# Down pages of experts 8 to 30 requested by ScalarE on its own queue, and another order of the last two experts

## What is computed

```python
def hierarchical_moe(x, wg, bg, we, be, w_gate, w_up, w_down):
    g_prob = softmax(xt @ wg + bg)                 # 4 groups of 8 experts
    g_top_p, g_idx = lax.top_k(g_prob, 1)
    e_top_l, e_idx = lax.top_k(e_logits, 2)        # two experts of that group
    gates = softmax(e_top_l) * g_top_p
    ...
    hb = silu(xb @ w_gate[e]) * (xb @ w_up[e])     # 1024 -> 512
    out = hb @ w_down[e]                           # 512 -> 1024
    ...
    return sum over each token's two experts of gate * out
```

## Time and profile before

| | us |
|---|---|
| three runs, median (lowest to highest) | 1268.96 (1267.98 to 1270.03) |
| the profiled execution | 1268.41 |
| its span, first to last instruction | 1266.7 |
| TensorE busy | 1040.9 (82%) |
| VectorE busy | 478.3 (38%) |
| ScalarE busy | 234.8 (19%) |
| chain that ended last: TensorE | 51% of the span |
| chain that ended last: DMA | 45% of the span |
| HBM traffic over the span | 364 GB/s |

### The profile page before, as it was taken

How to read it: one execution, slowest core, us unless ns; L and a number is a source line. 1 busy time by engine, 2 the same in 40 slices (tenths; PEclk the granted TensorE clock), 3 DMA queues, 4 the chain that set the end, 5 groups by cost and what they waited for, 6 DMA issues and landing times.

```text
span 1266.7 us, 22370 instructions
## 1 busy us (share of the span) xinstructions
PE 1040.9 (82%) x9525; PEld 704.6 (56%) x9525; DVE 478.3 (38%) x1230; ACT 234.8 (19%) x526; POOL 4.9 (0%) x27
## 2 busy tenths in 40 slices
PE   9999998866767575889999999999967675758676
PEld 7888755533433342448888888876533333425243
DVE  2342543532223222237665556464343222222223
ACT  2221121111111111103433333121111111111111
POOL 1000000000000000000000000000000000000000
PEclk9999998978788877899999999999988878878789
DMA  9888799999999999996676664899999999999997
GB/s 342 237 338 332 255 419 429 426 428 428 429 429 428 429 429 427 417 394 187 190 231 225 229 223 151 334 361 427 428 427 427 430 428 429 427 429 429 429 419 297
DMA packets 98305, 461.49 MB, mean 364 GB/s; under 512 B 17468, under 2 KB 60728, under 8 KB 73400
## 3 DMA queue, kind: packets, MB, share of 16 engines
q1 hardware_dynamic: 97872, 460.34, 90.5%
q10 hardware_dynamic: 360, 0.15, 0.0%
HBM read 459.38 MB, written 1.08 MB: 364 GB/s over the span
## 4 chain that ended last, share of the span: by engine, by line
PE 51%; DMA 45%; SPq 1%; DVE 1%; issue 1%; ACT 1%; POOL 0%; POOLq 0%; DVEq 0%; ACTq 0%
DMA front<-in_expert_w_up 39%; PE pa L1534 10%; PE pa L1829 8%; PE pb L1534 8%; DMA arena<-in_expert_w_down 5%; PE wa L1829 5%; PE acc L1565 4%; PE wb L1859 3%; PE acc L1684 2%; PE pb L1609 1%; SPq L362 1%; PE pb L1903 1%; PE wa L2124 1%; PE pb L1785 1%; PE acc L1869 1%
## 5 line engine op out<-in xcount | busy, mean ns | idle before, releaser
L1829 PE MATMUL pa<-front,arena 128*32 128x256 f32 x1792 | 126.6, 445 | 80.8 <-DMA front<-in_expert_w_up 80.8
L1289 DVE TENSOR_SCALAR lower<-lower 128x128 f32<-128x128 f32 x64 | 14.4, 225 | 417.6 <-ACT lower L606 417.6
L1829 PE MATMUL wa<-front,arena 128*32 128x256 f32 x1232 | 96.7, 479 | 88.5 <-DMA front<-in_expert_w_up 85.0
L1829 PEld LDWEIGHTS pa<-front,arena 128*32 128x32 f32 x1792 | 63.0, 128 | 146.9 <-DMA front<-in_expert_w_up 93.6
L1829 PEld LDWEIGHTS wa<-front,arena 128*32 128x32 f32 x1232 | 46.1, 136 | 142.1 <-DMA front<-in_expert_w_up 95.0
L606 ACT ACTIVATE arena<-wb 32x256 f32<-32x256 f32 (+2 forms) x236 | 88.9, 377 | 105.0 <-PE wb L1859 96.6
L1859 PE MATMUL wb<-w_dn,conv_raw 128*32 128x256 f32 x1472 | 87.9, 379 | 2.3 <-DMA w_dn<-in_expert_w_down 2.0
L1534 PE MATMUL pa<-hnT,w_x 128*128 128x256 f32 x384 | 85.1, 380 | 0.0
L1829 PE MATMUL wa<-w_x,arena 128*32 128x256 f32 x896 | 64.4, 451 | 19.1 <-DMA w_x<-in_expert_w_up 19.1
L1534 PEld LDWEIGHTS pa<-hnT,w_x 128*128 128x128 f32 x384 | 72.5, 190 | 10.0 <-issue 0.3
L1534 PE MATMUL pb<-hnT,w_x 128*128 128x256 f32 x336 | 74.5, 380 | 0.0
(11 more groups left out here) (345 smaller groups left out, 1252.0 us busy)
## 6 DMA issues: line engine op xcount, KB each, us to landing
w_dn<-in_expert_w_down SPq DMA_DIRECT2D x46, 2048.0 KB, 26.4
front<-in_expert_w_gate SPq DMA_DIRECT2D x42, 2048.0 KB, 19.1
front<-in_expert_w_up SPq DMA_DIRECT2D x42, 2048.0 KB, 23.6
w_x<-in_expert_w_gate SPq DMA_DIRECT2D x15, 2048.0 KB, 32.2
w_x<-in_expert_w_up SPq DMA_DIRECT2D x15, 2048.0 KB, 36.6
arena<-in_expert_w_down SPq DMA_DIRECT2D x14, 2048.0 KB, 25.8
w_x<-in_odd_in_proj SPq DMA_DIRECT2D x16, 1024.0 KB, 5.5
front<-in_expert_w_up SPq DMA_DIRECT2D x10, 1024.0 KB, 8.8
```

The source lines that it names most:

```text
L1289: link(v.tensor_scalar(eg, eg, 1.0, None, ALU.add))
L1829: ins = mm(gu[32 * j:32 * j + 32, :, :], xb[:, k, c0:c0 + CAP], w[k][:, :, P * j:P * j + P], start=(k == 0), stop=(k == KC - 1))
```

## The change

ScalarE gets a function `down_page(l, before)`. It asks, on ScalarE's own queue, for the down page that goes into the buffer of expert `before`, right after the copies of that expert's output. It covers positions 8 (`OWN`) to 30. SyncE keeps the down pages of positions 5 to 7 and of 31, and all gate and up pages; it no longer waits for down projections in between.

At the end of a layer SyncE asks for gate/up 30, then for gate/up 31 in two halves along the contraction (four of eight blocks each, gate and up of a half together), then for down 31. TensorE runs pass 29, down 28, down 29, sum 28, pass 30, sum 29, down 30, pass 31 in two halves with a wait each, sum 30, down 31, sum 31. The six warming matmuls are gone. ScalarE copies the output of position 30 after the Exp of 30, not after that of 31. The final norm's weights are asked for behind down 31 without the wait for its last half.

```diff
+OWN = 2 * QUAD
...
-                    for part in (2, 0, 1):
+                    for part in (2, 0, 1) if e < OWN else (0, 1):
                         expert_part(l, e, part, NE * l + previous(DSLOT if part == 2 else SLOT, e), which)
...
-                for parts in ((0, 1), (2,)):
-                    for e, which in last:
-                        for part in parts:
-                            expert_part(l, e, part, NE * l + previous(DSLOT if part == 2 else SLOT, e), which)
+                for part in range(2):
+                    expert_part(l, NE - 2, part, NE * l + previous(SLOT, NE - 2), last[0][1])
+                sp_.wait_ge(S["gu_done"], NE * l + previous(SLOT, NE - 1) + 1)
+                for half in range(2):
+                    k = slice(KC // 2 * half, KC // 2 * half + KC // 2)
+                    for part in range(2):
+                        w = (expert_w_gate, expert_w_up)[part][l, ds(last[1][1], 1), :, :]
+                        sp_.dma_start(w_gu[SLOT[NE - 1]][:, part, k, :],
+                                      w.rearrange("a (p k) f -> p (a k) f", k=KC)[:, k, :]
+                                      ).then_inc(S[("gu_res", "gu_in1")[half]], 16)
+                expert_part(l, NE - 1, 2, NE * l + previous(DSLOT, NE - 1), last[1][1])
...
-            sp_.wait_ge(S["dn_in3b"], 2 * uses(DSLOT, 3, NE) * 16)
...
+            def down_page(l, before):
+                for e in range(OWN, NE - 1):
+                    if previous(DSLOT, e) == before:
+                        which = act.value_load(order[0:1, NE * l + e:NE * l + e + 1], min_val=0, max_val=NE - 1)
+                        w = expert_w_down[l, ds(which, 1), :, :].rearrange("a (p j) n -> p (a j) n", p=P)
+                        d = DSLOT[e]
+                        dst = w_dn4 if d == 4 else w_dn[d]
+                        act.dma_start(dst[:, :, :], w).then_inc(
+                            (S["dn_in0"], S["dn_in1"], S["dn_in2"], S["dn_in2"], S["dn_in4"])[d], 16)
...
                         outputs_of(l, e - 1)
+                        if e - 1 != WIDE:
+                            down_page(l, e - 1)
...
-                    if e == NE - 1:
-                        output_alone(l, e - 1)
+                    if e == NE - 2:
+                        output_alone(l, e)
...
                         af(o_y, Y_ps, ACT.Copy).then_inc(S["w_act"], 1)
+                        down_page(l, WIDE)
...
+                    if e == NE - 1:
+                        pe.wait_ge(S["gu_res"], 48 * l + 48)
+                        gate_up(xs, CAP * j, gu_cols(s), GU[e % 2], ks=range(KC // 2))
...
+                    elif e == NE - 1:
+                        gate_up(xs, CAP * j, gu_cols(s), GU[e % 2], ks=range(KC // 2, KC)).then_inc(S["gu_done"], 1)
...
-                    if e and e != NE - 2:
+                    if e and e < NE - 2:
                         down_of(l, e - 1)
...
                     if e == NE - 2:
-                        warm(6)
+                        down_of(l, e)
```

More of the change, by code:

```diff
@@ L1975, in moe @@
                     if e == 3:
-                        pe.wait_ge(S["gu_res"], 16 * l + 16)
+                        pe.wait_ge(S["gu_res"], 48 * l + 16)
                     if e == WIDE:
```

## The result

The changed kernel takes 1280.16 us (four runs, 1276.47 to 1283.47) against 1269.49 us. The ratio is 1.0084, with an interval of 1.0068 to 1.0101: 10.7 us slower (8.6 to 12.8), where 2.5 us were forecast and 1277.0 us was the end of the range. The profiled execution took 1280.43 us, with a span of 1278.7 us, 12.0 us more than before.

A forecast was written before the change was run, and what follows sets the result against it. Bytes and rate bound the middle of a layer, with the slowest DMA engine setting its last landing. Terms 0.9 + 1.7 - 0.1 = 2.5 us, added to the median of 1268.96 us, gave 1271.5 us; range 1264.5 to 1277.0 us.

The forecast's parts named there:

- The rate: In the expert loop: traffic stays at about 429 GB/s, landings 29.3 us apart for two experts, last landing of each layer unmoved.
- the lateness: Mid-layer: overtaking down pages make gate/up 7.6 us later, paid once; pass 28 starts at 528.3 and 1219.0 us.
- the sharing: Two queues: even sharing (sum 2.6 us) or place by time of asking (1.7 us); the dearer, even sharing, was taken.
- The chain behind gate/up 30: Layer end: pass 30 to the last down pass takes 16.7 us; floor 0.9 us later in each layer.
- layer 0's delay goes on in full: Behind layer 0: its 0.9 us delay carries on, since TensorE's chain follows and the odd mixer's weights use the same queue.
- The norm's weights: Final norm: weights asked for behind down 31 bring back only 0.1 us, since VectorE also needs the first square sum.
- The start of pass 29 and its length: Layer ends: pass 29 starts at 541.5 and 1231.5 us; 10.2 and 10.5 us from there to pass 30, hardly any idle ahead.
- Rival 1: Layer ends: slower by low clock in pass 29 (1.5 us a layer) or late overflow look (1 us a layer); 13%.
- The dry stretch: Overflow look: gate/up 30 asked for at 538.8 us with 2.3 us of cover; failing that, up to 1 us a layer.
- Rivals 2: Experts 8 to 30: two queues feed the DMA engines better, 3.3 us at half a per cent, 6.7 at one; 15%.
- Rival 3: Two queues lower the rate through contention; half a per cent is 3.3 us more, 1274.8 us; 7%.
- Rival 4: Hardly any change: down pages keep place by asking time, filled overflow-look gap gains 0.7 us a layer; 0.3 us, 1269.3 us; 15%.

The follow-up runs named there:

- e6: The changed kernel with TensorE's overflow loop (skipped anyway, its list is empty) left out: 1273.64 us, ratio 1.0044 to the kernel before.
- e8: The kernel before with TensorE's overflow loop left out: 1270.13 us, ratio 1.0013.
- e2: The kernel before with only the down pages of experts 8 to 29 moved to ScalarE's queue, old order at the end: 1276.76 us, ratio 1.0045.
- e9: e2 with SyncE's wait for down 27 moved into the overflow loop, so the queue never runs dry: 1271.21 us, ratio 1.0027 to the kernel before.
- e12: The changed kernel with only SyncE's wait for down 27 moved into the overflow loop: 1278.51 us, ratio 1.0074 to the kernel before.
- e11: The changed kernel without SyncE's wait for down 27 when the overflow list is empty and without TensorE's overflow loop: 1273.25 us, ratio 1.0025 to the kernel before.
- e7: The kernel before with SyncE reading the overflow list's bounds ahead of its wait for down 27, the second bound once: 1269.33 us, ratio 1.0000.
- e5: The kernel before with SyncE also waiting for the weighted sum of quad 6 ahead of its overflow look: 1276.80 us, ratio 1.0064.
- e10: e9 with TensorE's overflow loop left out as well: 1269.30 us, ratio 1.0006 to the kernel before.

## Why the prediction was wrong

**The rate, the lateness, the sharing: right in the main, with luck in the closeness.** Traffic at 428 GB/s between 200 and 530 us in both kernels; pass 28 at 528.32 in place of the forecast 528.3; pass 29 of layer 0 at 541.51 in place of 541.5. The 7.6 us don't hold for every page: passes 26, 27 and 28 start 8.2, 4.0 and 7.6 us late. The eight kernels with two queues do the same up to there, and in their traces pass 28 of layer 0 starts anywhere from 524.9 to 530.7; that it met the forecast to a tenth is luck. That the two queues share about evenly was an assumption. The traffic of two stretches of 2 us of the changed kernel, 1218 to 1220 and then 1222 to 1224 us (packets, MB, share of the engines):

```profile
q10 hardware_dynamic: 30, 0.49, 57.5%
...
q1 hardware_dynamic: 32, 0.39, 46.3%
...
q1 hardware_dynamic: 31, 0.48, 55.8%
...
q10 hardware_dynamic: 21, 0.34, 40.3%
```

0.49 MB against 0.39, then 0.34 against 0.48: about even, as the round robin in the section "Queues, rings and completion order" of the Trainium skill, page "DMA: Bandwidth & Descriptors", has it. In layer 1 pass 28 came 1.5 us later than 1219.0 + 2.8 = 1221.8. That lies within the scatter between such traces; the pages no longer come evenly, and the rate of 427 GB/s would be 0.7 us of it. Which it is was not tried.

**The chain behind gate/up 30: right.** 16.7 us forecast from the start of pass 30 to the end of the last down pass; 16.5 us in layer 0 (553.82 to 570.33) and 16.8 us in layer 1 (1252.25 to 1269.05). That layer 0's delay goes on in full: right, 2.8 us. The norm's weights: right.

**The start of pass 29 and its length: wrong, and this is the step that failed.** The prediction wrote "now there is hardly an idle stretch ahead of it, so I take 10.2 and 10.5". It took the 3.64 us ahead of pass 29 in layer 1 for a wait for the page, which a late TensorE would not see. The row itself said otherwise: its reason is "issue" and not DMA, unlike its sister row in layer 0. It is TensorE's stop behind the skipped overflow code, gone with that code in e6. Such a stop comes after the work ahead of it, wherever that lies. The old kernel had it ahead of pages that landed about then, so it cost nothing (e8); the changed one has it on the chain. In layer 1 the 7.5 us that the sum lacks are: pass 28 1.5 us late, 4.5 us more between it and pass 29, and 1.5 us because the clock did fall in that idle stretch (5.16 us in place of 3.66). In layer 0 the 1.9 us are the stop inside pass 29. Together 9.4 us of the 9.5 us by which the profiled span missed the sum of 2.5 us.

Rival 1 was the nearest. It had the cold clock, but as a chance of its own and at 1.5 us; what brought it about, the stop behind the overflow code, was named nowhere. The forecast's own step to full clock in pass 29 held in layer 0 (3.23 and 0.64 us of matmuls) and failed in layer 1. The sum had the two ends of the sharing at 2.6 and 1.7 us; with the norm's 0.1 us taken off both they are 2.5 and 1.7, which changes nothing.

**The dry stretch: price wrong, small effect here.** The request of gate/up 30 came at 538.53, forecast 538.8. But "2.3 us of cover" counted from the landing of the slowest DMA engine, and most engines had run out from 537 on. The prediction capped the loss at 1 us per layer. Between e2 and e9 it was 3.0 us in layer 0. In the changed kernel it is 1.3 to 2.4 us in both layers together, not clear of nothing (e12, e6 and e11): the chain of TensorE ends the layer and hides most of it.

**Rivals 2, 3 and 4.** No rate was gained in any kernel, so 2 falls. Rival 3 is small in the changed kernel (428 and 427 GB/s against 428), but not wrong in kind: e12 was 0.9% lower in layer 0. Rival 4 falls with the sharing, and e7 shows no profit from a filled gap. The two parts add up within the noise: 5.7 us for the queue alone and 3.7 us for the end alone make 9.4 us, against 10.7 us (8.6 to 12.8).

## What to carry to other kernels

Before counting on an idle stretch to vanish, look at its reason: one that ends with "issue" behind a branch over code may be the engine waiting for its instructions, and then it moves along with the engine's work. Leaving the code out in one run tells. A queue's lead is not free to spend either: pages that overtake make the consumer late once, and every fixed stop and look behind it, so far hidden by the lead, comes onto the path. Where a transfer stream is the bound, the last requests must not wait for the consumer.

## What the runs showed of the hardware

- Behind the branch over a loop that never runs (some 270 instructions, two register loads ahead of it) TensorE stood still for 3.4 to 4.7 us in layer 1 while the DMA engines were busy, at most 2.2 us where they were nearly idle (e5), and not at all once the code was gone (e6, e10). In layer 0 it stood still for 1.2 to 1.9 us at the 57th matmul behind the branch, if it had not waited for a page before.
- A late look that left 7.6 us more out of a saturated stream cost 8.1 us (e5); filling a gap of 4.1 us in e2 brought the last page of layer 0 forward by 3.0 us (e9); filling gaps of 0.9 and 0.7 us brought nothing that can be told, 1.4 us at most (e7). That the DMA engines stand somewhat apart, and so fill small gaps, is how I read the last; it was not measured engine by engine.
- Two queues over the same engines never raised the rate: 428 GB/s over 330 us with one, 424 to 428 with two. They changed the order of landing: the gate/up passes of layer 0's loop in the changed kernel start 4 to 8 us late, unevenly.
